# Half of K as split products in five projection groups of the first layer, and three reorderings around the mLSTM heads

## The reference, cut to what matters

```python
h = rmsnorm(x, g_pre)
proj = h @ w_in                       # 256 x 1024 @ 1024 x 6144
q_a, k_a, v_a, g_a = proj[..., 0:aw], proj[..., aw:2*aw], proj[..., 2*aw:3*aw], proj[..., 3*aw:4*aw]
x_m, z_m = proj[..., 4*aw:4*aw+mw], proj[..., 4*aw+mw:]
o_a = moba_attention(heads(q_a), heads(k_a), heads(v_a), rel_bias)
y_a = o_a * silu(g_a)
x_c = silu(causal_depthwise_conv(x_m, conv_w, conv_b))
h_m = mlstm_chunkwise(q_m, k_m, v_m, i_pre, f_pre)     # 4 heads of 256
h_m = headwise_layernorm(h_m, mh_norm)
y_m = (h_m + skip * x_c) * silu(z_m)
x = x + rmsnorm(concat([y_a, y_m]) @ w_out, g_post)
```

## Time and profile before

| | |
|---|---|
| median of 3 runs | 2057.17 us |
| profiled execution, its own time | 2056.11 us |
| its span | 2054.3 us |
| TensorE busy | 2008.7 us, 98% |
| VectorE busy | 1622.5 us, 79% |
| ScalarE busy | 1274.8 us, 62% |
| DMA, mean | 267 GB/s |

### The profile page before, as it was taken

One profiled execution on the slowest core, in us unless ns is written; L12 is line 12 of the kernel. 1 busy time (PEld: TensorE's weight loads), 2 busy tenths in 40 slices (PEclk: granted clock), 3 DMA queues, 4 the chain that ended last, 5 costly groups with the idle time before them and its releaser, 6 DMA issues.

```text
span 2054.3 us, 29306 instructions
## 1 busy us (share of the span) xinstructions
PE 2008.7 (98%) x9820; PEld 1646.1 (80%) x9820; DVE 1622.5 (79%) x2257; ACT 1274.8 (62%) x1690; POOL 49.3 (2%) x60
## 2 busy tenths in 40 slices
PE   8999999999999999999999999999999999999998
PEld 7786779758888878888757888888888888888887
DVE  6456786786774886666658989899998989999898
ACT  2211356554443475455447888788888878888886
POOL 0000000000000000002000000000000000000000
PEclk9999999999999999999999999999999999999999
DMA  9777654356553335563328999999999999999996
GB/s 324 177 282 275 254 190 133 103 167 195 192 185 102 103 111 197 185 185 99 117 98 317 403 353 406 353 399 380 368 393 352 405 354 399 389 360 391 354 401 234
DMA packets 275462, 548.69 MB, mean 267 GB/s; under 512 B 29484, under 2 KB 81205, under 8 KB 275125
## 3 DMA queue, kind: packets, MB, share of 16 engines
q1 hardware_dynamic: 266189, 528.46, 70.2%
q0 software_dynamic: 3984, 14.68, 2.4%
q10 hardware_dynamic: 5208, 4.49, 1.2%
HBM read 537.11 MB, written 10.48 MB: 267 GB/s over the span
## 4 chain that ended last, share of the span: by engine, by line
PE 92%; DVE 5%; ACT 1%; issue 1%; DMA 0%; SPq 0%; DVEq 0%; ACTq 0%
PE sum L1657 13%; PE bank L1639 10%; PE bank L1641 10%; PE bank L1640 10%; PE bank L755 10%; PE bank L1237 7%; PE sum L1219 6%; PE bank L1239 3%; PE sum L817 2%; PE bank L771 1%; PE sum L1309 1%; PE bank L1625 1%; PE sum L797 1%; PE sum L1671 1%; PE sum L798 1%; PE sum L799 1%
## 5 line engine op out<-in xcount | busy, mean ns | idle before, releaser
L3222 DVE TENSOR_TENSOR x_lo<-ring,x_hi 128x1024 fp32r<-128x1024 f32 x672 | 780.3, 1221 | 44.3 <-ACT x_hi L2261 24.4
L2261 ACT ACTIVATE x_hi<-ring 128x1024 fp32r<-128x1024 f32 x648 | 667.0, 1058 | 119.1 <-PE bank L1641 66.1
L1639 PE MATMUL bank<-x_hi,hg_hi 128*128 128x512 f32 x896 | 354.2, 395 | 1.6 <-DVE xtr L3179 1.6
L1641 PE MATMUL bank<-x_hi,hg_lo 128*128 128x512 f32 x896 | 349.4, 390 | 0.0
L1640 PE MATMUL bank<-x_lo,hg_hi 128*128 128x512 f32 x896 | 348.9, 389 | 0.0
L2469 DVE TENSOR_TENSOR w_lo<-ring,w_hi 128x1024 fp32r<-128x1024 f32 x130 | 156.0, 1223 | 77.9 <-ACT w_hi L2024 76.9
L1237 PE MATMUL bank<-hT_hl,w_hi 128*128 128x512 f32 x608 | 215.6, 398 | 1.4 <-DVE hT_hl L2453 0.9
L2024 ACT ACTIVATE w_hi<-ring 128x1024 fp32r<-128x1024 f32 x130 | 136.8, 1059 | 126.0 <-PE sum L1219 66.3
L1641 PEld LDWEIGHTS bank<-x_hi,hg_lo 128*128 128x128 f32 x896 | 168.2, 188 | 35.8
L1639 PEld LDWEIGHTS bank<-x_hi,hg_hi 128*128 128x128 f32 x896 | 168.4, 188 | 34.9 <-DVE xtr L3179 1.7
L755 PE MATMUL bank<-hT,ring 128*128 128x256 f32 x864 | 192.4, 384 | 3.5 <-DMA ring<-in_w_in 1.8
(11 more groups left out here) (604 smaller groups left out, 2934.6 us busy)
## 6 DMA issues: line engine op xcount, KB each, us to landing
ring<-in_sw_we_gate SPq DMA_DIRECT2D x114, 1024.0 KB, 7.1
ring<-in_sw_we_up SPq DMA_DIRECT2D x112, 1024.0 KB, 7.5
ring<-in_sw_we_down SPq DMA_DIRECT2D x112, 1024.0 KB, 7.3
ring<-in_w_in SPq DMA_DIRECT2D x36, 1024.0 KB, 7.7
ring<-in_w_ff SPq DMA_DIRECT2D x32, 1024.0 KB, 5.3
ring<-in_ada_w SPq DMA_DIRECT2D x24, 1024.0 KB, 9.4
ring<-in_w_out SPq DMA_DIRECT2D x12, 1024.0 KB, 6.1
ring<-in_cv_w_gate SPq DMA_DIRECT2D x11, 1024.0 KB, 5.2
```

Source lines behind the costliest of these rows:

```text
L1639: mm(ps[b][:, :], hg_hi[:, k, :], hi[:, cols], start=(k == 0), stop=False)
L1641: last = mm(ps[b][:, :], hg_lo[:, k, :], hi[:, cols], start=False, stop=(k == KC - 1))
L2261: go(f(x_hi[:, hp % MSLOTS, :], ring[:, s, lo:lo + PIECE // 2], ACT.Copy), c.sig("hi_ready", hp))
L3222: v.tensor_tensor(x_lo[:, hp % MSLOTS, :], ring[:, s, lo:lo + PIECE // 2], x_hi[:, hp % MSLOTS, :].bitcast(F32), ALU.subtract).then_inc(c. ...
```

## The change

For the five groups 5632, 0, 512, 1024 and 1536 (`B1_MIXED`) a new function `cols_mixed` takes the place of `cols_T`. Chunks 4 to 7 of K stay float32 products. Chunks 0 to 3 become three fp32r products each: the weights' high part is made by ScalarE (`b1w_high`) in three slots of `d_hi`, the low part by VectorE (`b1w_low`), written over the weights in the ring. The tokens' high and low parts of chunks 0 to 3 are made once, early (`b1x_hi` in the place of `wide`, `b1x_lo` in unit 15). So the load of `g_post` into `wide`, and of a bias into unit 15 (`gm`), come later: after the last mLSTM output on ScalarE's queue, and after `moments` on GpSimd's, ahead of `rstd`.

`ada_sum(8)` moves ahead of the wait for `rstd` on VectorE, `ada_sum(9)` from between `mix_heads(1)` and `mix_heads(2)` to behind `mix_heads(3)`. TensorE turns heads 2 and 3 between the two tiles of group 2560, not behind them.

```diff
+B1_MIXED, B1_SLOTS = (5632, 0, 512, 1024, 1536), 3
...
-            def cols_tok(stage, name, col):
+            def cols_tok(stage, name, col, between=None):
                 w, keys = chunks(name, col)
                 for t in range(NT):
+                    if t and between:
+                        between()
...
+            def cols_mixed(col):
+                g, banks = B1_MIXED.index(col), [J.fill(pe, "b1p", col // 256)]
+                w, keys = chunks("w_in", col)
+                low = ring_r[:, W.place(("w_in", col, 0)), :].rearrange("p (k n) -> p k n", k=4)
+                for q in range(2):
+                    if q:
+                        banks.append(J.fill(pe, "b1p", col // 256 + 1))
+                    for k in range(4, KC):
+                        for j in range(2):
+                            mm(ps[banks[q]][:, j * S:(j + 1) * S], w[k][:, q * S + j * P:q * S + (j + 1) * P], hT[:, k, :],
+                               start=(k == 4 and j == 0), stop=False)
+                for half in range(2):
+                    hp = 2 * g + half
+                    pe.wait_ge(*c.at("b1w_low", hp))
+                    hi = d_hi[:, hp % B1_SLOTS, :].rearrange("p (k n) -> p k n", k=2)
+                    for q in range(2):
+                        for k in range(2):
+                            kk = 2 * half + k
+                            for j in range(2):
+                                o, cs = ps[banks[q]][:, j * S:(j + 1) * S], slice(q * S + j * P, q * S + (j + 1) * P)
+                                mm(o, hi[:, k, cs], b1x_hi[:, kk, :], start=False, stop=False)
+                                mm(o, hi[:, k, cs], b1x_lo[:, kk, :], start=False, stop=False)
+                                last = mm(o, low[:, kk, cs], b1x_hi[:, kk, :], start=False, stop=(kk == 3 and j == 1))
...
-            cols_T("b1p", "w_in", 5632)
+            cols_mixed(5632)
...
-                    cols_T("b1p", "w_in", 512 * i)
+                    cols_mixed(512 * i)
...
-            cols_tok("b1v", "w_in", 2560)
-            turn("mlstm", nrm, qs=(2, 3))
+            cols_tok("b1v", "w_in", 2560, lambda: turn("mlstm", nrm, qs=(2, 3)))
...
+            def b1w_high(g):
+                key = ("w_in", B1_MIXED[g], 0)
+                act.wait_ge(*W.ready(key))
+                for hp in (2 * g, 2 * g + 1):
+                    if hp >= B1_SLOTS:
+                        act.wait_ge(*W.ffn_used("b1w", hp - B1_SLOTS))
+                    lo = (hp % 2) * (PIECE // 2)
+                    go(f(d_hi[:, hp % B1_SLOTS, :], ring[:, W.place(key), lo:lo + PIECE // 2], ACT.Copy), c.sig("b1w_high", hp))
+
+            act.wait_ge(*J.full("vm", 1, 1))
+            act.wait_ge(*J.full("vec", 3))
+            do(f(b1x_hi.rearrange("p k n -> p (k n)"), hT[:, 0:4, :].rearrange("p k n -> p (k n)"), ACT.Copy), c.sig("b1x_high"))
             copy(aT[0:8, 0:S], ("gates",), S, rows=slice(0, 8))
-            act.dma_start(wide[:, :], everywhere(A["g_post"], D)).then_inc(c.sem("wide_in"), 16)
+            b1w_high(0)
...
             for q in (22, 23):
                 copy(pair(mix1, q - 20 + 4), ("b1p", q), func=ACT.Silu)
+            b1w_high(1)
...
                 probs_T("m", i, T384, "mO")
+                if i < MH - 1:
+                    b1w_high(2 + i)
 
             act.wait_ge(*J.full("mO", MH - 1))
+            act.dma_start(wide[:, :], everywhere(A["g_post"], D)).then_inc(c.sem("wide_in"), 16)
...
+            dve.wait_ge(*c.at("b1x_high"))
+            do(v.tensor_tensor(flat(b1x_lo[:, :, :]), flat(hT[:, 0:4, :]), flat(b1x_hi).bitcast(F32), ALU.subtract))
...
+            b1w_low(0)
             dve.wait_ge(*c.at("softplus", "gates"))
...
+                    b1w_low(1 + i)
                     ada_sum(4 + i)
...
+            ada_sum(8)
             dve.wait_ge(*c.at("rstd", "mlstm"))
...
-            ada_sum(8)
             ada(7)
...
-            ada_sum(9)
             mix_heads(2)
             mix_heads(3)
+            ada_sum(9)
             ada(8)
...
-            pool.wait_ge(*J.emptied("vec", 3))
+            pool.wait_ge(*c.at("moments"))
             pool.dma_start(gm, everywhere(A["ada_b_2"][:, 2 * D:3 * D], D)).then_inc(c.sem("gates_bias_in"), 16)
-            pool.wait_ge(*c.at("moments"))
```

More of the change, by code:

```diff
@@ L337, in program @@
         nrm = sb("nrm", NT, D)
+        with ExitStack() as phase:
+            wide_r = phase.enter_context(nc.sbuf_tensor("wide_r", [P, D], F32R))
         wide = sb("wide", D)
@@ L388, in program @@
             mix1_hi = mix3_low = sp_("mix1_hi", 8, S)
-            sp_("units_14_and_15", 2 * 1024, dt=F32)
+            sp_("unit_14", 1024, dt=F32)
+            unit_15 = sp_("unit_15", 4, S)
             d_hi = sp_("d_hi", SPLIT_SLOTS, PIECE // 2)
@@ L446, in program @@
         rows_hi[B1_ORDER_OUT[-1]] = (rows_hi_last[:, 1, :], rows_hi_odd[:, :])
+        b1x_hi, b1x_lo = wide_r[:, :].rearrange("p (k n) -> p k n", n=S), unit_15
         relbias = U(6, HEADS1, 384)
@@ L906, in ada_rows @@
                     done(mm(ps[b][:, :], ones, adasum[x % 4], start=True, stop=True), "ada", ADA[x])
+            def cols_mixed(col):
[21 more added lines that the diff above has]
+                                last = mm(o, low[:, kk, cs], b1x_hi[:, kk, :], start=False, stop=(kk == 3 and j == 1))
+                        if half:
+                            s = done(last, "b1p", col // 256 + q)
+                    if half == 0:
+                        s = c.sig("b1w_used", hp)
+                        last.then_inc(s.sem, 1)
+                    W.halves["b1w", hp] = (s.name, s.base)
+                free(keys, s)
             cols_T("b1p", "w_in", 4096, fresh="pre")
@@ L2575, in _, with b1w_low @@
             do(v.tensor_scalar(lg[:, :, 12:16], gl[:, :, 4:8], 0.0, None, ALU.min), go)
+            def b1w_low(g):
+                x = W.place(("w_in", B1_MIXED[g], 0))
+                for hp in (2 * g, 2 * g + 1):
+                    dve.wait_ge(*c.at("b1w_high", hp))
+                    cs = slice((hp % 2) * (PIECE // 2), (hp % 2 + 1) * (PIECE // 2))
+                    v.tensor_tensor(ring_r[:, x, cs], ring[:, x, cs], d_hi[:, hp % B1_SLOTS, :].bitcast(F32), ALU.subtract)\
+                        .then_inc(c.sig("b1w_low", hp).sem, 1)
+            b1w_low(0)
             dve.wait_ge(*c.at("softplus", "gates"))
```

## The result

The changed kernel takes 2047.47 us (median of 5 runs, 2045.90 to 2048.34), the kernel before 2057.17 in the same measurement (2056.48 to 2059.46). The ratio is 0.995, with a 95% interval of 0.9938 to 0.9962: 9.7 us faster, 7.8 to 12.8 by the interval. The forecast was 2050.8, and its range ended at 2047.8, 0.3 above what came. The profiled execution took 2047.63 us, with a span of 2045.8; its forecast was 2049.7.

The account below looks back on a forecast made before the run. TensorE, 92% of the chain that ended last, was taken to bound the kernel. Groups 5.6 plus heads 1.0 less softplus 0.2 gave 6.4 us off 2057.17: 2050.8, range 2047.8 to 2054.0.

Parts of the forecast that it names:

- The groups: Five groups on TensorE, each 12.7 us where it was 13.8: 5.6 us less in all, ends 3.9 and 6.0.
- The cover: Low parts and probabilities from VectorE ready before TensorE asks: no wait; thinnest cover in the loop 1.6 us.
- The first softplus: ScalarE's table load ahead of the first head shifts, delaying VectorE: 0 to 0.5 us lost, taken as 0.2.
- The heads: Heads turned between the tiles of group 2560: TensorE's 1.00 us wait ahead of group 3072 goes; ends 0 and 1.2.
- The clock: Dip in the first loop group, after the gate columns' pause, stays; 1.1 us less if missed, 1.1 more if another comes.
- The low end: Fast end of the range: 6.0 + 1.2 gained and the dip missed, 1.1, so 8.3 us less: 2047.8.
- The step from one profiled execution to the median: Median of the runs taken as 1.06 us above the profiled execution: 2049.7 profiled, 2050.8 median.
- C: TensorE waits at `b1w_low` or for the probabilities as long as a group became shorter: 2055 to 2057; chance 0.08.
- D: Unhidden weight load sets fp32r pace at 0.19 us in the groups, 11 us more in five: 2067; chance 0.04.
- B: A second clock dip, or a TensorE wait of 1 to 2.5 us counted as covered: 2052 to 2053.5; chance 0.18.

Follow-up runs that it names:

- before_k6: The kernel before with 6 idle float32 matmuls of 256 columns ahead of group 5632: 2056.51 us in one run.
- again: The changed kernel word for word, run once more for a second trace: 2048.93 us (5 runs), ratio 0.9962.
- sum8_back: The changed kernel with `ada_sum(8)` put back behind the normalisation: 2048.96 us.
- order_only: The kernel before with the three reorderings alone, all groups in float32: 2056.26 us (11 runs), ratio 0.9998.
- g_only: The changed kernel with its three reorderings undone, only the five mixed groups left: 2051.62 us (11 runs), ratio 0.9975.

## Why the prediction was right or wrong

**The groups: right.** 1.2 off the stage of group 5632, and the loop from 74.46 (before_k6, without a dip) to 69.66: 4.8. Together 6.0, where I took 5.6 and gave 6.0 as the larger end. That end had another reason, float32 records of 0.219 us, which didn't come, so meeting it was chance. The float32 half was 6.91 for 6.9; a split matmul 0.119 us for 0.121, and 48 times five times 0.002 is the difference.

**The cover: right, some terms too small.** No wait for the low parts or the probabilities; the cover of the latter is 2.1 for 1.6.

**The first softplus: the term of 0.2 lost was nothing.** The rows from gates to first head in the changed kernel, which answer to the earlier trace rows:

```profile
84.78 1.06 ACT L1841 ACTIVATE d_hi<-ring 128x1024 fp32r<-128x1024 f32 x1
84.79 0.36 ACTq L1848 DMA_DIRECT2D sinkb<-in_sw_sinks  x1
...
89.36 1.28 ACT L1853 ACT_TABLE_LOAD   x1 [2.57 <-issue]
...
101.57 0.92 PE L1017 MATMUL bank<-aT,consts 4*128 4x128 f32 x4 [0.65 <-DVE mcol L2652]
```

ScalarE's DMA issue starts 0.01 us behind the start of the copy and runs beside it, so the table comes at 89.36. With the 0.7 us by which this trace is ahead at the gates that is 90.1, earlier than either end that I gave (90.8 and 92.9). The pause is still 0.65.

**The heads: right in sum, wrong in one reason.** 0.9 for 1.0. I had costed the bias load on GpSimd at 0.66 and called it covered. It is covered, but with VectorE waiting it makes `rstd` 1.46 later; and I gave `ada_sum(8)`'s move nothing, where it is that very move that covers it (0.8 lost without it). The 1.0 is not the reordering of `mix_heads` alone.

**The clock: this step failed.** I wrote "The pause stays, so I let the dip stay", and allowed one dip of 1.1 to be missed or to come. Three things in it were wrong. The pause stays and the dip is often missed (there in 2 of 7 traces). The trace of before had a second dip, at the layer's end, in a row that I hadn't read, worth 1.3 us. And the size: 1.7 in the stage, of which 1.1 is in the group and the rest in the instructions ahead of it (`104.36 2.11` for the scores before, 1.51 in before_k6). The low end, made from 6.0 + 1.2 + 1.1, therefore ended at 2047.8. With both dips missed at their real size, 1.7 + 1.3 in place of 1.1, it would have stood at 2045.9, and the median at 2047.5 inside. Of the 3.3 us between forecast and median the terms of work are 0.5 (6.9 for 6.4); the rest is the clock, 1.6 to 1.8 by the two estimates above, and the scatter of medians. Chance has a part in it: the second measurement of the same code gave 2048.93, which lies inside the range.

**The step from one profiled execution to the median.** I added 1.06. It was the difference in one kernel between a single run and its median; in the changed kernel the profiled run (2047.63) and the median (2047.47) are the same. The number was chance, as the spans of 2045.8 and 2050.4 for the same code show; and the low end of the range took it off once more, 2048.9 less 1.1.

**The rivals.** C and D are refuted by the rows above (no wait; 0.12 us a matmul, in again):

```profile
111.35 0.12 PE bank L936
111.47 0.12 PE bank L937
```

D's price was too low for its own premise: a load hidden by nothing would come on top of a matmul, some 0.19 + 0.12 us (an estimate from the earlier trace rows), not 0.19 alone; 0.12 refutes both. B's waits didn't come in the changed kernel. A dip at the layer's end came in some of its traces, but the kernel before has that one too, so it didn't make the change worth less.

## What to carry to other kernels

Count the clock's dips in the trace of before, everywhere, behind pauses and behind runs of very small matmuls, and price each as something that a change may lose or gain merely by moving work in time; a sum of work was good to half a microsecond here (6.4 for 6.9) and the time still off by the dips. Compare the same stage in several traces of the same code before you give it a length. A step that is worth nothing by itself may be what covers another edit of the same change, so undo parts from the changed kernel too, not only add them to the one before.

## What the runs showed of the hardware

The same code, on the same chip, scattered from 2053.65 to 2060.72 us in 22 runs, and in the traces the difference between two executions is for the most part made of pieces of 1.2 to 1.7 us. At those that I looked at, the granted clock was 0.50 (1.2 GHz) over 3 to 7 us; a row that shows more also covers time at full clock. The pauses of 0.65 and of 2.73 us had it in some executions and not in others; 2.6 us of idle work ahead of them went with two dips fewer, and 1.7 us in the changed kernel went with both. One dip, near 740 us, came in all 14 traces with no pause ahead of it, behind 24 matmuls of 2 columns. What decides it was not found.

A DMA issue on GpSimd ahead of two small instructions took 0.71 us and 0.16 behind it, and with its later start made their end 1.46 us later (sum8_back against before). The two instructions took 2.82 us together while VectorE was summing rows (0.67 and 2.15, changed kernel) and 1.95 while it waited (0.26 and 1.69, sum8_back). The longer one took 2.15 in order_only as well, where VectorE sums and no DMA issue stands ahead, and 1.69 in before and g_only, where VectorE waits. So it goes with VectorE's work and not with the DMA issue; that the work beside it is the reason wasn't tested further.
